# Small loads behind the first weights, zero matmuls on TensorE ahead of x and in the router, and other ends of the dense feed-forward

## What is computed

```python
def hybrid(x):
    for i in range(2):
        mix = gated_deltanet(h, ...) if i == 0 else stick_breaking_attention(h, ...)
        h = layer_norm(ALPHA * h + mix)
        ff = swiglu(h, ffn...) if i == 0 else moe_swiglu(h, router, moe...)
        h = layer_norm(ALPHA * h + ff)

def gated_deltanet(x, w_in, conv_w, a_log, dt_bias, norm_w, w_out):
    proj = x @ w_in          # q, k, v (convolved), z, and 32 columns b, a
    ...
def swiglu(x, w_gate, w_up, w_down):
    return (silu(x @ w_gate) * (x @ w_up)) @ w_down      # inner width 3584

def moe_swiglu(x, router, w_gate, w_up, w_down):
    logits = x @ router                                  # 8 experts, the top 2 of each token
    y = sum over e of combine[:, e] * swiglu(x, w_gate[e], w_up[e], w_down[e])
```

## Time and profile before

| what | value |
|---|---|
| runs | 1642.95, 1645.74, 1642.7 us; median 1642.95 |
| profiled execution | 1646.35 us, span 1644.6 us |
| busy | PE 1598.4 us, DVE 1251.0, ACT 1010.5, POOL 109.4 |
| DMA | 467.58 MB, mean 284 GB/s |
| chain that ended last | PE 81%, DVE 9%, POOL 4% |

### The profile page before, as it was taken

One profiled execution on the slowest core, in us unless ns is written; L12 is line 12 of the kernel. 1 busy time (PEld: TensorE's weight loads), 2 busy tenths in 40 slices (PEclk: granted clock), 3 DMA queues, 4 the chain that ended last, 5 costly groups with the idle time before them and its releaser, 6 DMA issues.

```text
span 1644.6 us, 22481 instructions
## 1 busy us (share of the span) xinstructions
PE 1598.4 (97%) x8303; PEld 1351.1 (82%) x8303; DVE 1251.0 (76%) x976; ACT 1010.5 (61%) x899; POOL 109.4 (7%) x125
## 2 busy tenths in 40 slices
PE   8999999999999997999999999999999999999995
PEld 7899888788887996888888888888888888888884
DVE  5787467554546466998988988988887987987987
ACT  5755474533442564677766776776776776766763
POOL 1577010000000000300000000000000000000000
PEclk9998999999999998999999999999999999999998
DMA  7483227645554633999999999999999999999990
GB/s 242 161 297 108 99 82 277 230 163 194 183 201 143 214 128 103 333 395 385 385 380 344 375 385 344 375 387 344 378 382 338 388 383 344 380 381 338 379 389 36
DMA packets 204826, 467.58 MB, mean 284 GB/s; under 512 B 12016, under 2 KB 18416, under 8 KB 204784
## 3 DMA queue, kind: packets, MB, share of 16 engines
q1 hardware_dynamic: 200272, 460.39, 76.8%
q10 hardware_dynamic: 3808, 4.51, 0.9%
q0 software_dynamic: 704, 2.10, 0.3%
HBM read 457.51 MB, written 9.45 MB: 284 GB/s over the span
## 4 chain that ended last, share of the span: by engine, by line
PE 81%; DVE 9%; POOL 4%; issue 3%; ACT 2%; DMA 1%; SPq 0%; DVEq 0%; ACTq 0%; POOLq 0%
PE ps L1051 23%; PE ps L1053 23%; PE ps L1052 23%; DVE w_lo L1725 2%; PE ps L1463 2%; DVE w_lo_more L1725 2%; POOL X L522 2%; POOL ab L517 1%; PE ps L1079 1%; PE ps L1081 1%; PE ps L1082 1%; PE ps L1357 1%; DMA raw<-in_gdn_w_in 1%; DVE X L1771 1%; DVE stats L1757 1%
## 5 line engine op out<-in xcount | busy, mean ns | idle before, releaser
L1725 DVE TENSOR_TENSOR w_lo<-raw,w_hi 128x2048 fp32r<-128x2048 f32 x237 | 540.4, 2302 | 121.1 <-ACT w_hi L597 117.9
L597 ACT ACTIVATE w_hi<-raw 128x2048 fp32r<-128x2048 f32 x236 | 448.4, 1913 | 93.7 <-PE ps L1053 43.0
L1725 DVE TENSOR_TENSOR w_lo_more<-raw,w_hi_more 128x2048 fp32r<-128x2048 f32 x191 | 429.3, 2286 | 10.8 <-ACT w_hi_more L597 10.6
L597 ACT ACTIVATE w_hi_more<-raw 128x2048 fp32r<-128x2048 f32 x191 | 358.6, 1909 | 9.5 <-DMA raw<-in_moe_w_down 5.5
L882 ACT ACTIVATE hTh<-ps 128x512 fp32r<-128x512 f32 (+1 forms) x63 | 40.7, 645 | 302.6 <-PE ps L1463 302.6
L1051 PE MATMUL ps<-w_hi,xeh 128*128 128x512 f32 x480 | 187.6, 391 | 3.5 <-DVE xel L2186 2.1
L1053 PE MATMUL ps<-w_hi,xel 128*128 128x512 f32 x480 | 186.8, 389 | 0.0
L1052 PE MATMUL ps<-w_lo,xeh 128*128 128x512 f32 x480 | 186.8, 389 | 0.0
L1051 PE MATMUL ps<-w_hi_more,xeh 128*128 128x512 f32 x416 | 166.5, 400 | 0.0
L1053 PE MATMUL ps<-w_hi_more,xel 128*128 128x512 f32 x416 | 162.4, 390 | 0.0
L1052 PE MATMUL ps<-w_lo_more,xeh 128*128 128x512 f32 x416 | 162.2, 390 | 0.0
(11 more groups left out here) (341 smaller groups left out, 2764.1 us busy)
## 6 DMA issues: line engine op xcount, KB each, us to landing
raw<-in_moe_w_gate SPq DMA_DIRECT2D x112, 1024.0 KB, 7.9
raw<-in_moe_w_up SPq DMA_DIRECT2D x112, 1024.0 KB, 8.4
raw<-in_moe_w_down SPq DMA_DIRECT2D x112, 1024.0 KB, 7.4
raw<-in_gdn_w_in SPq DMA_DIRECT2D x23, 1024.0 KB, 6.3
raw<-in_ffn_w_gate SPq DMA_DIRECT2D x14, 1024.0 KB, 5.8
raw<-in_ffn_w_up SPq DMA_DIRECT2D x14, 1024.0 KB, 6.0
raw<-in_ffn_w_down SPq DMA_DIRECT2D x14, 1024.0 KB, 5.2
raw<-in_sb_w_in SPq DMA_DIRECT2D x12, 1024.0 KB, 5.4
```

The lines of the kernel that those rows point to most:

```text
L597: nc.scalar.activation(unit_hi(j), raw_slot(j), ACT.Copy).then_inc(hi_done, 1)
L1725: V.tensor_tensor(unit_lo(j), raw_slot(j), unit_hi(j).bitcast(F32), ALU.subtract).then_inc(lo_done, 1)
```

## The change

1. **Small loads.** ACT issues none at its start. SP issues `baw`, `cwr`, `dtb` and `negA` behind the load of unit 2; `small_in` counts these four. ACT issues `nw` and `rw` behind its `hi(3)`, on a semaphore of their own (`late_in`), for which POOL waits ahead of the first use of `nw` and ACT ahead of that of `rw`.
2. **Zeros first.** POOL clears the `zeros` tile as its first operation, and PE multiplies zeros 14 times (`busy(2, 14)`, 256 columns each) ahead of the transposes of x. The results are overwritten.
3. **Unit 1** is multiplied like unit 0: all 32 matmuls with its high part, which need `hi_done` alone, then 16 with its low part.
4. **Feed-forward.** The first transposes of the product stand between the two gate units of the next chunk; ACT makes `hi` of unit 6 and DVE `lo` of units 4 and 5 ahead of their parts of the first chunk. The zero matmuls L1495 go; the first down unit starts the sums itself. The first and the last turn of the loop are written out. In the last one the transposes stand between the two down units, and the split goes to new buffers, `hTh_last` and `hTl_last`.
5. **Router.** Zero matmuls stand behind the first logits (12), behind the last (5) and behind the transposes of the logits (16), and the clearing of banks 4 to 7 ahead of the ranks.

```diff
-SMALL = 16 * 6
+SMALL = 16 * 4
...
+        hTh_last = sb("hTh_last", [P, NT, 4, P], F32R, deep_units)
+        hTl_last = sb("hTl_last", [P, NT, 4, P], F32R, deep_units)
...
                         load(2 * c + half, 0, cols(gdn_w_in[0], half, CHUNK_COL[kind] + 512 * i), 4)
+                    if 2 * c + half == 2:
+                        sp.dma_start(baw, gdn_w_in[0, :, BA0:BA0 + 32].rearrange("(k p) n -> p k n", p=P)).then_inc(small_in, 16)
...
+            nc.gpsimd.memset(zeros[:].bitcast(F32), 0.0).then_inc(cst_step, 1)
             nc.gpsimd.memset(IDENT, 0.0).then_inc(cst_step, 1)
...
             pool.wait_ge(diag_done, 4)
+            pool.wait_ge(late_in, 32)
...
-            act.dma_start(baw, gdn_w_in[0, :, BA0:BA0 + 32].rearrange("(k p) n -> p k n", p=P)).then_inc(small_in, 16)
...
             hi(3)
+            act.dma_start(nw[:], gdn_norm_w[0].partition_broadcast(P)).then_inc(late_in, 16)
+            act.dma_start(rw[:], moe_router[0].rearrange("(k p) n -> p k n", p=P)).then_inc(late_in, 16)
...
+            act.wait_ge(late_in, 32)
...
-                hi(base + 4)
-                hi(base + 5)
+                for k in (4, 5, 6):
+                    hi(base + k)
                 hidden(dense, 0, hTh0, t)
...
+                chunk(0, hTh0, 1)
+                with act.Fori(1, FC - 2) as c:
+                    chunk(c, hTh0)
+                chunk(FC - 2, hTh_last)
...
-            def stationary_first(bank, xh, xl):
+            def stationary_high_first(j, bank, xh, xl):
...
+                    if j == 0:
+                        pe.wait_ge(first_hi, k + 1)
+                    elif k == 0:
+                        pe.wait_ge(hi_done, j + 1)
...
+                pe.wait_ge(lo_done, units(j))
...
+            def busy(bank, count):
+
+                for _ in range(count):
+                    nc.tensor.matmul(ps[:, bank, 0:256], zeros[:, 0:P], zeros[:], start=True, stop=True)
+
+            pe.wait_ge(cst_step, CST_ZEROS)
+            busy(2, 14)
...
-                if j == 0:
-                    stationary_first(bank, xT0h, xT0l)
+                if j < 2:
+                    stationary_high_first(j, bank, xT0h, xT0l)
...
-                for bank in y_banks:
-                    for quarter in range(4):
-                        nc.tensor.matmul(ps[:, bank + quarter // 2, quarter % 2 * 256:quarter % 2 * 256 + 256],
-                                         zeros[:, 0:P], zeros[:], start=True, stop=True)
...
+                pe.wait_ge(S["s"], 2)
+                wide(base + 4, 0, 0, g_banks, xTh, xTl)
+                turned(0)
+                wide(base + 5, 0, 1, g_banks, xTh, xTl)
+                up(0)
+                down_unit(0, 0, True)
+                down_unit(0, 1)
+                turned(1)
...
+                with pe.Fori(1, FC - 2) as c:
+                    gate_up(c)
+                    down_unit(c, 0)
+                    down_unit(c, 1)
+                    turned(c + 1)
+
+                gate_up(FC - 2)
+                down_unit(FC - 2, 0)
+                turned(FC - 1)
+                down_unit(FC - 2, 1)
                 pe.wait_ge(S["hl"], FC + 1)
...
             logits(0, 1)
+            busy(1, 12)
...
             logits(1, 1).then_inc(R_pe.sem, 1)
+            busy(1, 5)
...
+            busy(4, 16)
+            clear(range(4, 8))
             pe.wait_ge(R_dve.sem, R_dve.after("mask"))
...
-            clear(range(4, 8))
             pe.wait_ge(R_dve.sem, R_dve.after("pick1"))
...
-                lo(base + 2)
-                lo(base + 3)
+                for k in (2, 3, 4, 5):
+                    lo(base + k)
                 hidden(dense, 0, units(base + 3), hs0, u)
-                lo(base + 4)
-                lo(base + 5)
+                lo(base + 6)
                 hidden_lo(dense, 0, hTh0, hTl0, u)
```

More of the change, by code:

```diff
@@ L76 @@
 SB_CHUNKS = [(2, 0), (0, 0), (1, 0), (0, 1), (1, 1), (2, 1)]
-CST_IDENT = 2
+CST_ZEROS = 1
+CST_IDENT = 3
 CST = 15
-SMALL = 16 * 6
+SMALL = 16 * 4
 class Stages:
@@ L887, in ffn, with chunk @@
                 silu(dense, 0, units(base + 1), hs0, g)
-                hi(base + 4)
-                hi(base + 5)
+                for k in (4, 5, 6):
+                    hi(base + k)
                 hidden(dense, 0, hTh0, t)
-                with act.Fori(0, FC - 1) as c:
-                    for k in range(6):
+                def chunk(c, hTh, k0=0):
+                    for k in range(k0, 6):
                         hi(base + 6 + k, c)
@@ L895, in ffn @@
                             silu(dense, c + 1, units(base + 5, c), hs0, g)
-                    hidden(dense, c + 1, hTh0, t)
+                    hidden(dense, c + 1, hTh, t)
+                chunk(0, hTh0, 1)
+                with act.Fori(1, FC - 2) as c:
+                    chunk(c, hTh0)
+                chunk(FC - 2, hTh_last)
                 hi(base + 6, FC - 1)
@@ L1497, in ffn, with up @@
-                with pe.Fori(0, FC - 1) as c:
-                    chunk(base + 4, c, c + 1, True)
+                def up(c):
+                    pe.wait_ge(S["hl"], c + 2)
+                    wide(base + 6, c, 0, u_banks, xTh, xTl)
+                    wide(base + 7, c, 1, u_banks, xTh, xTl)
+                wide_first(base, 1, g_banks, xTh, xTl, transpose_normalized(0, (2, 6)))
+                wide(base + 2, 0, 0, u_banks, xTh, xTl)
+                wide(base + 3, 0, 1, u_banks, xTh, xTl)
@@ L1593, in logits, with clear @@
                 return last
+            def clear(banks):
+                for bank in banks:
+                    nc.tensor.matmul(ps[:, bank, 0:2], zeros[:, 0:P], zeros[:, 0:2], start=True, stop=True)
             turned(0, 1)
@@ L1614, in _ @@
             nc.tensor.matmul(ps[:, 3, 0:NE], ONES, mask[:, 1, :], start=False, stop=True).then_inc(R_pe.sem, 1)
-            def clear(banks):
-                for bank in banks:
-                    nc.tensor.matmul(ps[:, bank, 0:2], zeros[:, 0:P], zeros[:, 0:2], start=True, stop=True)
             def expert_rows(r, half):
@@ L2089, in ffn, with chunk @@
                 u = slice(2, 4)
-                lo(base + 2)
-                lo(base + 3)
+                for k in (2, 3, 4, 5):
+                    lo(base + k)
                 hidden(dense, 0, units(base + 3), hs0, u)
-                lo(base + 4)
-                lo(base + 5)
+                lo(base + 6)
                 hidden_lo(dense, 0, hTh0, hTl0, u)
-                with dve.Fori(0, FC - 1) as c:
-                    for k in range(6):
+                def chunk(c, hTh, hTl, k0=0):
+                    for k in range(k0, 6):
                         lo(base + 6 + k, c)
@@ L2100, in ffn @@
                             hidden(dense, c + 1, units(base + 7, c), hs0, u)
-                    hidden_lo(dense, c + 1, hTh0, hTl0, u)
+                    hidden_lo(dense, c + 1, hTh, hTl, u)
+                chunk(0, hTh0, hTl0, 1)
+                with dve.Fori(1, FC - 2) as c:
+                    chunk(c, hTh0, hTl0)
+                chunk(FC - 2, hTh_last, hTl_last)
                 lo(base + 6, FC - 1)
```

57 lines of the change are left out of this document (21 added, 36 removed).

## The result

| | before | changed |
|---|---|---|
| runs shown with the result, median | 1644.35 us (1642.7, 1642.95, 1645.74, 1647.74) | 1629.87 us (1628.11, 1628.98, 1630.75, 1631.2) |
| ratio | | 0.9909, 95% interval 0.9888 to 0.9929 |
| profiled execution | 1646.35 us, span 1644.6 | 1628.11 us, span 1626.3 |

The change is faster by 14.5 us by the medians (11.7 to 18.4 by the interval), and 18.2 us by the two profiled executions. The forecast was 14.5, 1628.5 us. Where the same code gets another clock in another execution, I call what one execution got its draw.

What follows compares the result with a forecast made beforehand. The expert stage was taken as dense, so only PE's idle and half-speed time ahead of it could be won: start 5.5, feed-forward 5.0, router 4.0, together 14.5 us, median 1628.5 us, range 1625.5 to 1636.5.

Steps and rivals of the forecast that it cites:

- its stream bounds it: Rival, expert stage: PE coming 4 us sooner only waits for loads, the router's 4.0 is lost, 1632.5 us; chance 0.09.
- Part 1: Start: moved small loads, zeros and unit 1's new order bring the small projection sooner by 5.5 us (3.2 to 6.2).
- ACT's copies start 0.4 us sooner: Start: ACT's first copies come at about 5.2 us, helping unit 0 start at 8.6 instead of 9.43.
- Each held about 16 matmuls at half speed: Start: units 0 and 1 each ran about 16 matmuls at half speed, 1.5 us too much.
- PE and ACT hardly working: Start: reading of one window before unit 1's arrival, whose stream ran at 200 GB/s.
- Part 2: Dense feed-forward: waits and zero matmuls at its first chunk and last pair go, 5.0 us (4.0 to 5.1).
- Part 3: Router: zeros hold PE's clock and clearing moves ahead, 4.0 us gained (bounds +4.3 and -1.7).
- PEclk falls in the router all the same: Router: sign named beforehand that the forecast is wrong, PE's clock dropping despite the zero matmuls.
- zeros do not hold the clock: Rival, start and router: PE still falls to half speed, gain only 6.5 us, 1636.4 us; chance 0.13.
- start's gain absorbed: Rival, mixer: POOL's chain or the two late loads use up the start's gain, 1634 us; chance 0.06.
- slower by starving small loads: Rival, start: small loads starve behind SP's large ones, ACT and PE wait; landing at 40 gives 1648.4 us; chance 0.02.
- every wait of the mixer is on work that starts from here, so the gain moves on whole: Mixer, after 26.40 us: waits depend on engine work that shifts too, so the start's 5.5 us carries through.

Runs made afterwards that it cites:

- e1: The kernel before with the dense feed-forward's part of the change alone; median 1638.49 us, ratio 0.9964.
- e4: The kernel before with the router's part alone (three groups of zero matmuls, clearing moved ahead); median 1639.51 us, ratio 0.9982.
- e7: The changed kernel with the six small loads issued by ACT at the start again, as before; median 1631.99 us, ratio 0.9918.
- e8: The changed kernel itself, unchanged, measured a second time; median 1629.45 us, ratio 0.9900.
- e10: The changed kernel with unit 1 multiplied in its old order, needing its low part from the first matmul on; median 1632.98 us, ratio 0.9925.
- e12: The changed kernel with zero matmuls in two more idle gaps (10 in the mixer, 4 in the router), second execution; 1629.04 us, ratio 0.9895.
- e3: The kernel before with the start's whole part alone, zeros included; median 1639.51 us, ratio 0.9970.
- e9: The changed kernel without the router's three groups of zero matmuls, the clearing still early; median 1634.16 us, ratio 0.9928.

## Why the prediction was right, point by point

**What bounds the kernel**: right. The experts' stage kept its length to 0.3 us (18.6 ahead at its first matmul, 18.3 at the end), and everything came from ahead of it. The rival that its stream bounds it falls by the same lengths of 986.7 to 987.4 us in all fourteen profiles.

**Part 1, 5.5 us (3.2 to 6.2)**: 6.0 between the two profiles, 4.1 to 4.4 (4.3 below) against the two executions of the old start without a fall. The arrivals were right (unit 1 at 12.32, small loads by 16.3 where "near 17" was said, no wait ahead of unit 1's high part, small projection at 20.4 where "near 21" was said). Three steps were not. "ACT's copies start 0.4 us sooner" failed: they start at 5.53, behind the zeros, and unit 0 gains by faster transpositions (2.24 us for 3.88) instead. "Each held about 16 matmuls at half speed" took both falls for the rule, where e1 and e4 had neither. The one in unit 1 was worth 1.5 us: it took 7.34 us from its first matmul to the small projection's, and 5.85 in e1 and e4. The one in unit 0 was worth nothing in the old order, which waited for unit 1's low part at 18.7 to 19.1 either way. And "PE and ACT hardly working" misreads the window at 200 GB/s: PE was busy for 0.13 of it, ACT for 0.83; the arrival of 12 that was taken does not hang on it. The Trainium skill's sentence that I had set beside this ("TensorE: Matmul & The Clock Gate", Part 1: the gate runs free of the kernel's start, and runs differ) is borne out by the traces: of the same code's matmuls some 16 each of units 0 and 1 were slow in the execution of before and none in e1 and e4, and the small projection began at 26.43, 24.83 and 24.57 us. The other sentence from the Trainium skill ("DMA: Bandwidth & Descriptors", Rules for kernel authors: another queue brings no bandwidth) is not tested by itself, since no run moves a load from queue to queue at the same place. That the place in the stream counts is shown: unit 1 landed at 14.3 to 14.7 us with the small loads in front and at 11.5 to 13.2 without.

**Part 2, 5.0 us (4.0 to 5.1)**: 5.8, outside its own bounds, in every profile. The mechanism was right and the term mis-sized: the idle column and the zeros, 2.66 + 2.37, leave out what a stop costs beside the idle time. Two rows of before, to be held against the earlier trace rows and the changed kernel's above:

```profile
303.97 0.39 PE L1053 MATMUL ps<-w_hi,xTl 128*128 128x512 f32 x1
...
508.40 1.03 PE L1463 MATMUL ps<-cst,hs 128*128 128x128 f32 x8
```

Counted from the start of the last matmul ahead to the second behind, the first place went from 4.24 us (303.97 to 308.21) to 1.35 (299.09 to 300.44), 2.89; the end from 3.98 (508.17 to 512.15) to 1.34 (489.48 to 490.82), 2.64, and another 0.24 ahead of the transpositions at 521.71. Most of the surplus lies ahead of the stop's end: from the last matmul to the transposes 1.70 us became 0.24, 0.15 more than the 1.31 of idle time, and from the transposes to the next down unit 3.41 became 0.80, 0.24 more than the 2.37. The idle column counts from a modelled end, 0.39 us behind a matmul's start, where the next one could have started after 0.23. The first matmul behind the stop isn't it: it takes 0.34 us to the next one's start, but 0.31 to 0.32 in the changed kernel too, where nothing stops ahead of it.

**Part 3, 4.0 us (+4.3 to -1.7)**: 3.9 in five of nine kernels with the zeros (e4, e7, e8, e10, e12), 2.3 in the four others, in which the clock fell once during the pick passes. Both are against the profile of before; against e1 to e3 they are 0.3 less. "If the zero matmuls hold the clock" is right up to the ranks, in all nine; for the pick passes it is right in about half of the draws. The terms are right one by one: logits 0.65 for 0.6 (635.92 to 647.38 before, 619.59 to 630.39 now), ranks and clearing 1.21 for 1.25 (3.01 to 1.80), of which e9 shows 0.6 for the clearing, picks and copies 2.05 for 2.3 (7.35 before, 5.30 in e4). What I had named as the proof that I was wrong, "PEclk falls in the router all the same", did occur in the first profile, and cost 1.6 us, not the 5.7 of the rival (4.0 less -1.7), because it fell for 3.4 us and not for 13.7. (The delays in that rival's sum, 0.7, 0.5 and 1.5 less 0.9, make 1.8 and not 1.7, which changes nothing.)

**The sum** of the parts as they were measured is 4.3 to 6.0 + 5.8 + 2.3 to 3.9, 12.4 to 15.7 us; 14.5 lies inside, by terms that erred up and down (5.5 for 4.3 to 6.0, 5.0 for 5.8, 4.0 for 2.3 to 3.9), which is luck as much as method. The 18.2 of the profiled pair is that and a good draw in the mixer. **The rivals**: *zeros do not hold the clock* falls by e9 in the router, and at the start by nine kernels of ten with unit 0 at full speed, against two of four without zeros; *start's gain absorbed* falls, the 6.0 us of 26 us stand unchanged at 147 us; *slower by starving small loads* falls, the slowest of the four that ACT waits for took 10.3 us from its issue, and they had landed by 16.3, though SP's issue of one stood 5.6 us in a full queue. What the forecast lacked is the mixer: "every wait of the mixer is on work that starts from here, so the gain moves on whole" holds for waits, but its speed is drawn anew in each execution, 31.9 to 39.1 us over all kernels, 33.3 and 39.1 in two executions of the changed one. In one pair of executions that can be as much as any of my three terms; the medians over several, and the range of 1625.5 to 1636.5, leave less of it.

## What to carry to other kernels

Where PE runs in small passes or between waits, take a stage's length from several executions before a gain of a few us is given to an edit; the same instructions laid side by side in two traces show at once which stage moved, and the unchanged stage that moved here was the clock's doing. Zero matmuls pay where they fill idle time ahead of dense work that is then really there (1.3 to 2.6 us at the start, against one execution without; 3.0 to 4.6 in the router); ahead of dense runs of tiny passes no gain was shown here, and strewn singly among them they cost three and a half times their length. A stall costs 0.15 to 0.24 us beside the idle time that the profile shows.
